# Moving the split activations by 64 bytes and spacing the gathered expert rows by 16 bytes in a two-layer hybrid trunk

## The reference

```
for l in (0, 1):
    h = rms_norm(x, g_mix[l]);  u = h @ w_in[l]
    merged = sum over the mixers of sigmoid(gate) * (mixer(u) @ w_branch[l])
    x = x + merged @ w_out[l]
    h = rms_norm(x, g_ffn[l])
    x = x + (swiglu(h, w1, w3, w2) if l == 0
             else sum_e gate_e * swiglu(h, w1[e], w3[e], w2[e]))
```

## Time and profile before

| what | value |
|---|---|
| median of two runs | 1742.53 us (1741.94 to 1743.11) |
| span of the profiled execution, first to last instruction | 1738.7 us |
| what lies outside of the span, median less span | 3.8 us |
| mean granted TensorE clock over the span | 0.987 |
| TensorE matmul busy | 1689.6 us, 97% |
| TensorE weight load busy (overlaps) | 1454.0 us, 84% |
| VectorE busy | 1283.2 us, 74% |
| ScalarE busy | 1053.3 us, 61% |
| read from HBM | 450.74 MB |

### The profile page before, as it was taken

How to read it: one execution, slowest core, us unless ns; L and a number is a source line. 1 busy time by engine, 2 the same in 40 slices (tenths; PEclk the granted TensorE clock), 3 DMA queues, 4 the chain that set the end, 5 groups by cost and what they waited for, 6 DMA issues and landing times.

```text
span 1738.7 us, 25143 instructions
## 1 busy us (share of the span) xinstructions
PE 1689.6 (97%) x9630; PEld 1454.0 (84%) x9630; DVE 1283.2 (74%) x1078; ACT 1053.3 (61%) x902; POOL 51.5 (3%) x52
## 2 busy tenths in 40 slices
PE   7999989999899998999999999999999999999998
PEld 7988889999898888788788788788788788788787
DVE  5964754444696475787887887887887887887886
ACT  5544444444554445677677677677677677677675
POOL 0131000000013000000000000000000000000000
PEclk9999999999999998999999999999999999999999
DMA  9533445555353342699899899899899899899893
GB/s 331 172 123 105 142 142 170 193 174 165 122 170 122 116 141 86 253 369 342 316 363 335 323 366 329 333 364 329 319 375 330 327 368 331 324 370 330 322 373 146
DMA packets 231292, 452.46 MB, mean 260 GB/s; under 512 B 6992, under 2 KB 80720, under 8 KB 231120
## 3 DMA queue, kind: packets, MB, share of 16 engines
q1 hardware_dynamic: 231248, 451.82, 73.5%
HBM read 450.74 MB, written 1.05 MB: 260 GB/s over the span
## 4 chain that ended last, share of the span: by engine, by line
PE 89%; DVE 8%; issue 2%; ACT 1%; DVEq 0%; DMA 0%; ACTq 0%
PE bank L269 27%; PE bank L271 27%; PE bank L270 27%; DVE w_low L259 3%; PE bank L1237 2%; PE bank L1253 1%; DVE xacc L929 1%; PE bank L997 1%; DVE h_full L690 1%; PE bank L1087 1%; DVE gate L685 1%; DVE h_full L616 0%; PE bank L1106 0%; ACT w_high L255 0%; DVE rinv L606 0%
## 5 line engine op out<-in xcount | busy, mean ns | idle before, releaser
L259 DVE TENSOR_TENSOR w_low<-raw,w_high 128x2048 fp32r<-128x2048 f32 x427 | 975.5, 2290 | 323.8 <-ACT w_high L255 322.8
L255 ACT ACTIVATE w_high<-raw 128x2048 fp32r<-128x2048 f32 x427 | 818.3, 1917 | 441.6 <-PE bank L271 439.6
L269 PE MATMUL bank<-w_high,hg_high 128*128 128x512 f32 x896 | 358.5, 400 | 7.6 <-DVE w_low L259 7.6
L270 PE MATMUL bank<-w_low,hg_high 128*128 128x512 f32 x896 | 353.9, 395 | 0.0
L271 PE MATMUL bank<-w_high,hg_low 128*128 128x512 f32 x896 | 353.9, 395 | 0.0
L269 PE MATMUL bank<-h_high,w_high 128*128 128x256 f32 x1056 | 307.3, 291 | 9.4 <-DVE h_low L611 4.8
L270 PE MATMUL bank<-h_low,w_high 128*128 128x256 f32 x1056 | 300.9, 285 | 0.0
L271 PE MATMUL bank<-h_high,w_low 128*128 128x256 f32 x1056 | 300.9, 285 | 0.0
L269 PEld LDWEIGHTS bank<-h_high,w_high 128*128 128x128 f32 x1056 | 204.8, 194 | 15.0 <-issue 9.6
L269 PEld LDWEIGHTS bank<-w_high,hg_high 128*128 128x128 f32 x896 | 169.3, 189 | 47.6 <-DVE w_low L259 9.7
L270 PEld LDWEIGHTS bank<-h_low,w_high 128*128 128x128 f32 x1056 | 205.0, 194 | 1.6 <-issue 1.4
(11 more groups left out here) (225 smaller groups left out, 1587.8 us busy)
## 6 DMA issues: line engine op xcount, KB each, us to landing
raw<-exp_w SPq DMA_DIRECT2D x336, 1024.0 KB, 5.2
raw<-w_in SPq DMA_DIRECT2D x42, 1024.0 KB, 5.1
raw<-ffn_w SPq DMA_DIRECT2D x33, 1024.0 KB, 5.2
raw<-w_out SPq DMA_DIRECT2D x8, 1024.0 KB, 5.3
raw<-w_br_attn SPq DMA_DIRECT2D x4, 1024.0 KB, 4.9
raw<-w_br_pool SPq DMA_DIRECT2D x2, 1024.0 KB, 5.2
raw<-w_br_conv SPq DMA_DIRECT2D x2, 1024.0 KB, 5.4
cst<-consts SPq DMA_DIRECT2D x1, 1280.0 KB, 13.5
```

What stands on the lines that cost most here:

```text
L255: nc.scalar.activation(wh[c % SPLIT][:], raw[c % RAW][:], ACT.Copy).then_inc(s["high_done"], 1)
L259: nc.vector.tensor_tensor(wl[c % SPLIT][:], raw[c % RAW][:], wh[c % SPLIT][:].bitcast(F32), ALU.subtract).then_inc(s["split_done"], 1)
L269: pe.matmul(dst, lh, rh, start=start and i == 0, stop=False)
L270: pe.matmul(dst, lh, rl, start=False, stop=False)
```

## The change

A tile of 64 bytes that nothing uses is declared between `h_full` and `h_high`. Every tile declared behind it starts 64 bytes later: h_high, h_low, g_high, g_low, ht, perm, zero and hg now start 64 bytes past a multiple of 128, and y_high and y_low, which were 64 past one, at a multiple. raw, w_high, w_low, xT and h_full stay. The chunks of hg_high and hg_low get 132 columns of room in place of 128, so that a chunk starts 528 bytes behind the one before it, 16 bytes more than its 128 columns take; the writer and the reader address the first 128 columns. Tiles behind hg_low move by another 256 bytes.

```diff
+SHIFT = 16
+STAGGER = 4
...
         hf = sb("h_full", [P, KC, S])
+        sb("line_shift", [P, SHIFT])
         hH = sb("h_high", [P, KC, S], F32R)
...
-        hgH = sb("hg_high", [P, KC, P], F32R)
-        hgL = sb("hg_low", [P, KC, P], F32R)
+        hgH = sb("hg_high", [P, KC, P + STAGGER], F32R)
+        hgL = sb("hg_low", [P, KC, P + STAGGER], F32R)
...
-                    dst = (hgH if g < 2 else hgL)[:, 4 * (g % 2):4 * (g % 2) + 4, :]
+                    dst = (hgH if g < 2 else hgL)[:, 4 * (g % 2):4 * (g % 2) + 4, 0:P]
...
-                            (hgH[:, 4 * half_ + k, :], hgL[:, 4 * half_ + k, :], H[:, k, :], L[:, k, :]) for k in range(4)],
+                            (hgH[:, 4 * half_ + k, 0:P], hgL[:, 4 * half_ + k, 0:P], H[:, k, :], L[:, k, :]) for k in range(4)],
```

## The result

The changed kernel took 1720.88 us (1720.29 to 1721.46, two runs) against 1742.53: a ratio of 0.9882, 95% interval 0.9853 to 0.9911. That is 21.6 us, or 1.2%, where 44.5 had been forecast; the interval leaves no doubt of a gain, but it stays short of the two per cent border. The profiled execution's span fell from 1738.7 to 1719.4 us, by 19.3. The two differences are not the same because of the 3.8 us by which the median of before stood above its span: in every run of a whole kernel recorded from here on, the time is some 2.1 us above that run's own span (1721.46 over 1719.4 for the changed kernel). So the execution of before that was profiled was one of the quicker ones, near 1740.8 us.

A forecast was written before the change was run, and what follows sets the result against it. TensorE's product spacing was taken to bound the kernel; -18 - 3 + 0.5 - 12 - 12 = -44.5 us on the 1738.7 us span gave 1694.2, plus 3.8 made 1698 us, range 1658 to 1738 (8 in 10).

The forecast's parts named there:

- Step 1: Mixers and dense stage: h moving from 0 to 64 shortens its products' spacing as for y; -18 us, between -7 and -22.
- Step 4: Expert stage: g moving to 64 loses half the 19.1 ns excess, 9.5 ns per 512-column product; -12 us.
- Step 5: Expert stage: staggered hg slices lose a quarter of the 19.1 ns excess, 4.8 ns per product; -12 us.
- What bounds the kernel: Whole kernel: the chain of waits is 89% TensorE, so only the spacing between starts of successive products can pay.
- the offset between the two streams sets the spacing: TensorE at full clock: moving data and weight load disturb each other by their offset; excess 6.5 to 19.1 ns per product.
- Step 2: Dense stage: g moving to 64 takes its products from 118.8 to 113.2 ns; -3 us, between -0.5 and -3.
- Step 3: y moving from 64 to 0 slows its products from 113.2 to 120.0 ns, mostly covered by VectorE and ScalarE; +0.5 us.
- 512-column products do not follow the 256-column ones: Expert stage: named as one of two conditions that would make the prediction wrong; no size given.
- The 3.8 us outside of the span: Whole kernel: the earlier runs' median exceeded the profiled span by 3.8 us, which was added to 1694.2.
- only 256-column products gain: Rival: the experts' 512-column excess has another source, so only the first stages gain 20.5 us; 1722 us, chance 0.22.
- the slower rival: Expert products lock onto a longer spacing of 240 ns, +29 us; 1751 us in all, chance 0.10.

The follow-up runs named there:

- experiment 1: Shift without stagger: the changed kernel with the hg chunks packed again at 512 bytes; 1713.81 us, ratio 0.9845.
- experiment 3: The kernel before with a 64-byte idle tile ahead of everything, so weights and activations all move by 64; 1740.99 us, ratio 0.9999.
- experiment 4: Bare loops of products alone, operand offsets swept in steps of 16, then 4 bytes; 113.3 to 122.9 ns with 256 columns, 226.6 to 245.8 with 512.
- experiment 5: The kernel before with h moved to 192 bytes past the weights modulo 256, y put at 192; 1724.43 us, ratio 0.9901.
- experiment 6: The kernel before with hg alone moved inside its tile: by 128 bytes 1729.07 us (0.9928), by 28 bytes 1750.00 us (1.0048).
- experiment 7: Bare loop of products, each block behind one matmul of 20 to 204 columns that shifts the start; at 192, blocks at 113.3 and 117.9 ns.
- the sweep: The bare-loop runs of experiment 4: only products, with the address difference between moving and stationary operand varied; spacings in ns, no kernel time.
- the first sweep: Bare loop, offsets 0 to 496 bytes in steps of 16, 128-column matmuls ahead of each block; e.g. 120.0 ns at 0, 113.3 at 192 (256 columns).
- The second sweep: Bare loop, offsets within 256 bytes in steps of 4, 64-column matmuls ahead of each block; with 256 columns 128 gave 118.6 ns.

## Why the prediction went wrong

By place, the first stages gave 13.5 us of the 20.5 forecast, the experts 5.8 of the 24. The mechanism was right; two sizes were not. Step 1 took h at 64 for y at 64, and steps 4 and 5 took the price of a 512-column product from 256-column ones.

- *What bounds the kernel, and that only spacings count*: right. The chain, the counts and the waits stayed, and the difference is found in spacings and, between the two profiled executions, 3.6 us of clock.
- *That the offset between the two streams sets the spacing*: right as far as it goes, and shown by experiments 1, 3, 4, 5 and 6; the start has its part too, by experiment 7. The Trainium skill's sentence that the next weight load "doesn't steal SBUF read bandwidth from the running matmul" (page "TensorE: Matmul & The Clock Gate", section "Step-by-step: what each phase is for") would leave no room for this, as the prediction said. With these float32r products 28 bytes of difference cost 8 us of kernel time, and moving both operands together cost nothing. That it is read bandwidth which is lost is not shown.
- *Step 1, h at 64 taken to be like y*: this step failed. The caution named in it (y lies at 192 modulo 256, h would lie at 64) was the point. The period is 256 bytes, 64 has the 117.8 rhythm in 23 of 24 starts, 192 in 12. The term was -18 us and measured -8.4.
- *Step 2*: right. Dense g moved from 128 to 192 and got 113.3; the -3 measured -2.5.
- *Step 3*: y went to 120.0 as said. That its stage hides this was only argued from the chain; no run put y alone elsewhere.
- *Step 4, half of the excess goes with 512 columns*: this failed most, with step 5. I carried a ratio from one shape to another without a row for it. In the sweep the two shapes have different patterns: 64 is no better than most with 512 columns, and the best of all differences leaves 13.3 of the 19.1 ns. g, which counted modulo 256 went to 192 and not to 64, got 3.6 ns of the 9.5; -12 measured -4.6. The prediction had named this as a sign of being wrong: 512-column products do not follow the 256-column ones.
- *Step 5, the stagger takes a quarter off*: the reasoning that it visits good and bad places alike was right, the price was not. The mean over the places is 231.7, not 227.6; -12 measured -1.5. The change would have been 6 us better without it (experiment 1).
- *The 3.8 us outside of the span*: the later runs have 2.1, so the sum should have given 1696. This is small, and makes the forecast no better.
- *The rivals*: "only 256-column products gain", 1722 us, came within 1 us of the measured time by luck: its first stages gain 20.5 us where 13.5 were measured, its experts nothing where 5.8 were, since 512 columns do follow the difference. A longer spacing than 232 exists (242.9 at 156), so the slower rival was a real mechanism at another difference.

## What to carry to other kernels

Where TensorE's products follow each other without a gap, read the spacing of the starts before asking for fewer of them: here 120.0 or 113.3 ns for one and the same product of 256 columns, and 232.4 or 226.7 for one of 512, were worth some 40 us together, for a few bytes of padding. Sweep the difference between the moving and the stationary operand in a bare loop for each shape in use, several starts to each difference, and take one whose rhythm does not depend on the start, for the shape that has the most products; do not carry the answer from one shape to another. A stagger averages over good and bad places, so a fixed difference at the best place beat it here.

## What the runs showed of the hardware

- The spacing depends on the difference of the two operands' addresses modulo 256 bytes: 113.3 to 122.9 ns with 256 columns, 226.6 to 245.8 with 512, 111.4 to 111.8 (no dependence) with 128. At the half clock the excess is absent: 213 ns with 256 columns, and 427 ns for hg products of 512 columns near 693 us in the trace of before.
- There are several steady rhythms at one difference, chosen by the start and kept for whole runs: 113.3 or 117.8 at 192, 226.7 or 242 to 246 at 156. Which one the start picked depended on the length of the matmul ahead; no rule for it was found.
- The dense stage's g at 128 gave 118.8 where the first sweep has 120.0. The second sweep, from another start, has 118.6 there, so the start may explain it. The chunk pitch of its weights is another too (4096 bytes against 1024); that the pitch matters is a guess, not tried by itself. Nor was the distance between the high and the low tile, which was a multiple of 256 bytes in both sweeps.
- The Trainium skill's N / 2.4 + 2.5 ns (page "TensorE: Matmul & The Clock Gate", section "Back-to-back issue gap"), which the page calls the gap of an isolated matmul and which makes 109.2 and 215.8 ns here, was reached at no difference. The best were 113.3 and 226.6.
- Which part of the memory's or the array's structure makes the period of 256 bytes stays open; the runs show the dependence, not its cause.
